# Summing the squares of the pre-norm on VectorE at all seven boundaries of a hybrid decoder trunk

## The reference

```python
def rms_norm(x, g):
    xf = x.astype(jnp.float32)
    y = xf * lax.rsqrt(jnp.mean(xf * xf, axis=-1, keepdims=True) + EPS)
    return (y * g.astype(jnp.float32)).astype(x.dtype)
...
    x = x + 0.5 * rms_norm(swiglu(rms_norm(x, f1_pre), f1_wg, f1_wu, f1_wd), f1_post)
    h = rms_norm(x, m_pre)
    z = h @ w_in            # three groups of channels: short conv, spatial gating, Conformer conv
...
    x = x + rms_norm(mix, m_post)
    x = x + 0.5 * rms_norm(swiglu(rms_norm(x, f2_pre), f2_wg, f2_wu, f2_wd), f2_post)
    gate = jax.nn.sigmoid(rms_norm(x, e_pre) @ e_wg)
    x = x + rms_norm(gate * (p @ e_wp), e_post)
```

## Time and profile before

| | |
|---|---|
| median of 3 runs | 2665.72 us (2664.89 to 2725.86) |
| profiled execution | 2664.45 us |
| its span, slowest core | 2662.7 us (cores 2655.2 to 2662.7) |
| granted clock, cores | 0.992 to 0.994 |
| PE, PEld busy | 2552.5, 1677.8 us |
| DVE, ACT, POOL busy | 1132.0, 1090.5, 613.8 us |

### The profile page before, as it was taken

The page is one execution under the profiler, slowest core; times in us unless marked ns, Lnnn a source line. Parts: engine busy times, 40 slices in busy tenths (PEclk is TensorE's granted clock), DMA queues, the critical chain, the costliest instruction groups (busy, mean ns, idle before and its releaser), DMA issues.

```text
span 2662.7 us, 52925 instructions; the slowest of 8 cores (2655.2 to 2662.7 us)
## 1 busy us (share of the span) xinstructions
PE 2552.5 (96%) x18352; PEld 1677.8 (63%) x18576; DVE 1132.0 (43%) x2680; ACT 1090.5 (41%) x2220; POOL 613.8 (23%) x943
## 2 busy tenths in 40 slices
PE   6999999999999999999999999999989999999996
PEld 3676565666566666666566765667656676566764
DVE  2222775215621368321662137722174215772237
ACT  3123673125611376322741237722274124761236
POOL 0052232004305223100420412400051222240014
PEclk9999999999999999999999999999999999999998
DMA  8354252434335524233655542533343444334341
GB/s 164 58 94 82 41 96 49 75 66 83 53 76 91 93 43 89 48 70 66 124 124 96 114 89 37 93 64 65 63 80 64 83 70 83 42 72 80 61 83 65
DMA packets 54595, 205.43 MB, mean 77 GB/s; under 512 B 10656, under 2 KB 23744, under 8 KB 39456
## 3 DMA queue, kind: packets, MB, share of 16 engines
q0 software_dynamic: 32608, 178.81, 38.2%
q1 hardware_dynamic: 21728, 23.23, 3.1%
HBM read 372.17 MB, written 9.63 MB: 143 GB/s over the span
## 4 chain that ended last, share of the span: by engine, by line
PE 90%; DVE 3%; ACT 3%; issue 3%; DMA 1%; POOL 1%; DVEq 0%; SPq 0%; ACTq 0%; POOLq 0%
PE PS L614 88%; PE PS L620 2%; ACT L490 1%; DVE XT L656 1%; ACT SCR L645 1%; DVE R L663 0%; ACT SQS L645 0%; DMA RING<-W 0%; DMA XT<-xT 0%; DVE SCR L663 0%; POOL R L651 0%; DVE SCR L656 0%; ACT R L645 0%; ACT PS L645 0%; POOL XT L656 0%
## 5 line engine op out<-in xcount | busy, mean ns | idle before, releaser
L614 PE MATMUL PS<-R,RING 128*128 128x256 bf16 (+2 forms) x10439 | 1602.3, 310 | 52.0 <-ACT SCR L645 23.9
L614 PEld LDWEIGHTS PS<-R,RING 128*128 128x128 bf16 x10560 | 1030.7, 98 | 556.1 <-issue 75.2
L645 ACT ACTIVATE SCR<-PS 128x256 f32<-128x256 f32 (+2 forms) x818 | 372.3, 463 | 965.6 <-PE PS L614 948.9
L614 PE MATMUL PS<-HIDR,RING 128*128 128x256 bf16 (+2 forms) x4934 | 752.8, 309 | 10.0 <-ACT SQS L645 3.5
L656 DVE TENSOR_TENSOR HIDR<-SCR,PS 128x512 bf16<-128x512 f32 (+2 forms) x552 | 282.3, 512 | 873.2 <-PE PS L614 856.5
L614 PEld LDWEIGHTS PS<-HIDR,RING 128*128 128x128 bf16 x4992 | 487.4, 98 | 252.3 <-issue 3.3
L685 POOL DMA_DIRECT2D RING<-W x192 | 106.5, 555 | 1585.7 <-PE PS L614 1526.8
L645 ACT ACTIVATE SQS<-PS 128x256 bf16<-128x256 f32 (+2 forms) x288 | 131.4, 456 | 436.9 <-PE PS L614 432.6
L656 POOL TENSOR_TENSOR XT<-XT,SCR 128x256 f32<-128x256 f32 (+2 forms) x221 | 206.0, 941 | 270.1 <-DVE SCR L663 246.0
L663 DVE SCALAR_TENSOR_TENSOR R<-XT,VECT,PS 128x256 bf16<-128x256 f32 (+2 forms) x368 | 186.0, 564 | 65.7 <-ACT PS L645 53.2
L490 ACT ACT_TABLE_LOAD x163 | 209.1, 1283 | 2.9
(11 more groups left out here) (92 smaller groups left out, 1063.4 us busy)
## 6 DMA issues: line engine op xcount, KB each, us to landing
RING<-W POOLq DMA_DIRECT2D x116, 1024.0 KB, 8.6
RING<-W POOLq DMA_DIRECT2D x64, 704.0 KB, 6.1
RING<-W POOLq DMA_DIRECT2D x8, 768.0 KB, 6.5
XT<-xT SPq DMA_DIRECT2D x8, 512.0 KB, 10.9
XT<-xT SPq DMA_DIRECT2D x16, 256.0 KB, 9.0
yT<-SCR SPq DMA_DIRECT2D x16, 256.0 KB, 3.2
yT<-SCR SPq DMA_DIRECT2D x32, 128.0 KB, 2.2
RING<-W POOLq DMA_DIRECT2D x4, 512.0 KB, 5.1
```

What stands on the lines that cost most here:

```text
L614: S.add("pe", lambda e: e.matmul(out.build(), lhsT.build(), rhs.build(), start=start, stop=stop), r=[lhsT, rhs], w=[out], dur=max(n, 64) / ...
L645: return e.activation(out=out.build(), in_=in_.build(), func=func, **k2)
```

## The change

`boundary` gets a parameter `fold`. All three places that call it (the feed-forwards, the mixer and the embedding stage) pass `fold=True`. Then block 0's square is left where it is; at block 1 DVE adds the squares of blocks 0 and 1 into the fp32 statistics bank in PSUM; at blocks 2 to 5 it adds the next square to that; at block 6 it adds the bank to block 6's square and writes the sum in bf16 over that square, and a ones-matmul of it starts the accumulation; block 7's square gets the second ones-matmul. So six adds on DVE stand in for six of eight matmuls on PE. The adds have the boundary's priority and can go to DVE only. The statistics bank is taken by the first add and no longer by the first matmul.

```diff
-        def boundary(si, ys, Y, gains, nxt, g, eps=EPS):
+        def boundary(si, ys, Y, gains, nxt, g, eps=EPS, fold=False):
...
                     SQ_(Hs(si, m), Xs(si, m), n, (1, g), tag="xsq")
-                    MM(bv(st2, 0, n), fx(ONESB[:]), Hs(si, m), n, m == 0, m == KC - 1, (0, g), acq=[st2] if m == 0 else (), tag="stat")
+                    A_ = bv(st2, 0, n)
+                    if not fold:
+                        MM(A_, fx(ONESB[:]), Hs(si, m), n, m == 0, m == KC - 1, (0, g), acq=[st2] if m == 0 else (), tag="stat")
+                    elif m == 1:
+                        TT_(A_, Hs(si, 0), Hs(si, 1), ALU.add, n, (1, g), acq=[st2], tag="xsum")
+                    elif 1 < m < KC - 2:
+                        TT_(A_, Hs(si, m), A_, ALU.add, n, (1, g), tag="xsum")
+                    elif m == KC - 2:
+                        TT_(Hs(si, m), Hs(si, m), A_, ALU.add, n, (1, g), tag="xsum")
+                        MM(A_, fx(ONESB[:]), Hs(si, m), n, True, False, (0, g), tag="stat")
+                    elif m == KC - 1:
+                        MM(A_, fx(ONESB[:]), Hs(si, m), n, False, True, (0, g), tag="stat")
...
-                boundary(si, ys, Ys, gains_post, nxt, downs[KC - 1].g + skew(si) + 0.5)
+                boundary(si, ys, Ys, gains_post, nxt, downs[KC - 1].g + skew(si) + 0.5, fold=True)
...
-                boundary(si, ys, Ys, lambda m, l=l: vec(l, G_MPOST + m), (l, G_F2PRE), wO[1].g + skew(si) + 0.5)
+                boundary(si, ys, Ys, lambda m, l=l: vec(l, G_MPOST + m), (l, G_F2PRE), wO[1].g + skew(si) + 0.5, fold=True)
...
-                boundary(si, ys, Ys2, lambda m, l=l: vec(l, G_EPOST + m), nxt, wG[1].g + sk + 0.5, 4.0 * EPS)
+                boundary(si, ys, Ys2, lambda m, l=l: vec(l, G_EPOST + m), nxt, wG[1].g + sk + 0.5, 4.0 * EPS, fold=True)
```

## The result

| | before | with the change |
|---|---|---|
| median | 2666.2 us | 2675.14 us |
| span of the profiled execution | 2662.7 us | 2673.7 us |
| granted clock of the cores, mean | 0.992 to 0.994 | 0.983 to 0.987 |

The ratio is 1.0033, 95% interval 1.0024 to 1.0042: some 9 us slower, where 5 us faster was forecast. Within 2% it is the same kernel, but the interval leaves no doubt of the sign, and the time lies just above the upper end of the range given (2675). In some executions the cores of a die ran at a lower granted clock and took longer, up to 3016 us here; the medians of this table are of all executions, while every ratio, and every time from here on, leaves such executions out.

What follows compares the result with a forecast made beforehand. It took sub-tile 0's DVE chain to bound the mixer and embedding boundaries, PE most other stretches. 36.8 us removed less 13.2, 6.6, 7.4 and 4.8 left 4.8 us less: 2661 us, range 2644 to 2675.

Steps and rivals of the forecast that it cites:

- my rest: At the boundaries, losses set against the removed matmuls: 13.2, 6.6, 7.4 and 4.8 us for the four kinds.
- the clock: Rival: longer waits at the four mixer boundaries lower the granted clock, some 1.4 us each, +6, 2667 us; chance 0.05.
- A matmul's price: At all boundaries, 0.216 us from start to start at 512 columns; removal gives at most 36.8 us.
- Lost matmuls: At boundaries in stretches where PE waits anyway, removed matmuls give nothing: 16 us of the 36.8.
- stalls by the adds: At boundaries, DVE adds delay PE: 2.0 us at each of six critical places, 0.5 in eight other stages.
- Mixer to second feed-forward: Four boundaries where sub-tile 0's chain already sets the end: loss 3.3 us each, 13.2 in all.
- Embedding to next feed-forward: Two boundaries before the next layer's first feed-forward, sub-tile 0's chain likewise critical: loss 3.3 us each, 6.6 in all.
- second feed-forward to embedding: Four boundaries; sub-tile 0 gains, sub-tiles 1 and 2 lose their 1.35 us plus 0.5 stall: loss 1.85 each, 7.4.
- first feed-forward to mixer: Four boundaries; sub-tile 0 hidden, half of 1.35 us lost plus 0.5 stall: loss 1.2 each, 4.8 in all.
- PE-bound after all: Rival: all adds fall into gaps or replace residual adds moved to POOL; 21 us gained, 2645 us; chance 0.22.
- DVE's queue sets the end: Rival at sub-tile 0's boundary: nothing moves, no gap is used; 3.7 us at six places, 2683 us; chance 0.22.
- The first add's contention: At each boundary's first add, two SBUF operands slow POOL by at most 1.05 us; 6.3 at six places, about cancelling.

Runs made afterwards that it cites:

- feed-forwards only: The change with squares summed on DVE only at the eight boundaries behind the feed-forwards, mixer and embedding keeping eight matmuls: 2655.02 us, 0.9963 of before.
- mixer only: The change with squares summed on DVE only at the four boundaries behind the mixer: 2678.29 us, 1.0051 of the kernel before.
- embedding only: The change with squares summed on DVE only at the two boundaries behind the embedding stage: 2667.74 us, 1.0011 of the kernel before.
- no adds: The change without its six adds, six of eight ones-matmuls still left out, so the statistic holds blocks 6 and 7 alone: 2634.50 us, 0.9866 of before.
- adds beside all matmuls: The change with all eight ones-matmuls kept and six adds into another bank that nobody reads: 2688.52 us, 1.0077 of the kernel before.
- mixer, sub-tile 0 only: The change with squares summed on DVE only behind the mixer and only for sub-tile 0: 2682.97 us, 1.0060 of the kernel before.
- the change with fillers: The change plus twelve unread ones-matmuls behind sub-tile 0's two statistic matmuls, after each mixer and embedding: 2662.69 us, 1.0006 of the kernel before.
- The opposite choice: The change with DVE sums only for sub-tile 0 behind feed-forwards and sub-tiles 1 and 2 behind mixer and embedding: 2641.14 us, 0.9919 of before.
- the chain put ahead in DVE's queue: The change with sub-tile 0's products, sums and adds into h behind a mixer ahead of other sub-tiles' work on DVE: 2687.47 us, 1.0079 of before.

## Why the prediction was wrong

The balance of spans, in us, with the clock loss and the rest as defined above; "my rest" is the loss that the prediction set against the same boundaries.

| kernel | span | removed | clock loss | rest | my rest |
|---|---|---|---|---|---|
| feed-forwards only | -8.7 | -21.0 | +2.4 | 9.9 | 12.2 |
| mixer only | +14.1 | -10.5 | +7.8 | 16.8 | 13.2 |
| embedding only | +4.4 | -5.3 | +2.1 | 7.6 | 6.6 |
| the change | +11.0 | -36.8 | +16.8 | 31.0 | 32.0 |
| no adds | -28.2 | -36.8 | +3.4 | 5.2 | 16.0 |
| adds beside all matmuls | +24.2 | 0 | +5.4 | 18.8 | 16.0 |
| mixer, sub-tile 0 only | +17.7 | -5.2 | +5.6 | 17.3 | |
| the change with fillers | -4.2 | -36.8 | +2.9 | 29.7 | |

By the means of the eight cores the rest is 8.1, 16.8 and 5.5 us for the three parts, 31.1 for the change, 5.4 without adds and 17.5 beside all matmuls.

**The step that failed is the clock.** The prediction's sum of waits and lost cover, 32.0 us, comes out (31.0, as a remainder); the 15.8 us between its span of 2657.9 and the measured 2673.7 are the clock loss of 16.8 less that 1.0. I had it as a rival, at 4 x 1.4 = 5.6 us and a chance of 0.05, sized from one stretch and independent of the waits that my own forecast lengthened. Both were mistakes. By my own terms the waits behind the four mixers would grow from about 1 to about 4 us, so a fall of the clock there belonged into the forecast, not into a rival. And 1.4 us is the loss in one stretch; behind the first mixer of the kernel after, the stretches at 380 and 404 us lose 1.7 and 2.0, and there are such places behind both embeddings and inside the embedding stage near 1344 us as well. That the fillers take back 13.9 us of it (10.8 by the means of the cores), and 11 us of the time, is the test of this. The Trainium skill has the mechanism (TensorE: Matmul & The Clock Gate, HAM oscillation — how this bites in real kernels): a kernel whose waits for operands make TensorE throttle pays again at half rate after each. The rows agree, with 0.51 behind a wait of 3.44 us and 0.50 behind one of 2.69, but not for every wait: the one of 2.94 us in the kernel before left the clock at 1.00.

**A matmul's price: right.** 36.8 us by the distance of 0.216 us. The opposite choice gained 16.5 to 26.9 us for 18.4 counted, and removal alone some 30 of 36.8 (interval 23 to 48). The busy means, 78 us, would have been far off; PE's busy time fell by 4.9 us only (50 or more were forecast), because it is a union of overlapping records, the slow clock stretches it, and the trace of before misses 224 of its 18576 matmuls.

**Lost matmuls: too high; stalls by the adds: too low.** I had split the 32.0 into 16 of matmuls in stretches that wait anyway and 16 of stalls. Without adds the rest is 5, not 16. The adds alone, beside all eight matmuls, make 19, and in the change they make 26 more than without them, for 16. The errors cancelled. That the sum came out is therefore partly luck.

**Mixer to second feed-forward: place and sign right, too small.** The wait before the first up matmul was forecast near 4 us and is 3.44, 3.44, 2.69 and 2.69. The stretch was to be 25 us long; it is 30:
```profile
372.90:402.85 29.95, 22.76 (x180) 17.29 (x177) 28.36 (x59) 20.53 (x54) 17.67 (x18) 0.91 0.49 94
```
It begins 3.2 us earlier, about what the one boundary ahead of it has saved (2.65), and ends 3.9 later. DVE is busy for 28.36 of 29.95 us, with 59 operations instead of 41. Its timeline shows how 3.7 us of adds can lengthen the chain by 4.6 (sub-tile 0 alone) to 7:
```profile
391.83 0.73 DVE L663 SCALAR_TENSOR_TENSOR SCR<-R,VECT,PS 128x512 f32<-128x512 f32 x1
392.49 0.43 DVE L656 TENSOR_TENSOR PS<-SQS,PS 128x272 f32<-128x272 bf16 x1
392.83 0.68 DVE L656 TENSOR_TENSOR PS<-R,PS 128x512 f32<-128x512 bf16 x1
393.43 0.42 DVE L656 TENSOR_TENSOR SQS<-SQS,PS 128x272 bf16<-128x272 bf16 x1
393.78 0.68 DVE L656 TENSOR_TENSOR PS<-R,PS 128x512 f32<-128x512 bf16 x1
394.38 0.41 DVE L656 TENSOR_TENSOR PS<-SQS,PS 128x256 f32<-128x256 bf16 x1
394.71 0.73 DVE L663 SCALAR_TENSOR_TENSOR SCR<-R,VECT,PS 128x512 f32<-128x512 f32 x1
```
Between two products of sub-tile 0 there now stand two of its own adds and three of the other sub-tiles' sums for the post-norm, which come due in the same stretch, and the product is held by the whole queue. Sub-tile 0's fourth product starts at 385.98 us and the last two at 396.91; before, they ran from 386.72 to 393.43. I had also let one of its two residual adds move to POOL (1.1 us); over the kernel 31 did, so that 84 instead of 115 are on DVE, but in this stretch the two of 512 columns stayed. A count over the whole kernel was right and the critical place got none of it. The gaps that were to take 0.6 us are filled: DVE waits for nothing before the four middle adds at 512 columns (0.0 in the group).

**Embedding to next feed-forward, second feed-forward to embedding, first feed-forward to mixer.** 7.6 us for 6.6 and 9.9 for 12.2: right within what a profile can tell.

**The rivals.** "PE-bound after all" falls. "DVE's queue sets the end" describes the place and the wait best; its price beyond the forecast was paid as clock and not as further waits. The point from which it decides, 2.8 us for the chain instead of 2.0, is passed at the mixer (4.6 measured in the kernel that changes nothing else).

**The first add's contention.** I had looked for it on POOL's side only, at 1.05 us and about cancelled. It fell on DVE (up to 2.77 us for 0.69), and it cost the change nothing, because at the six places that I had counted it the add took 0.69.

What stays open: how much of the 26 us by which the adds lengthen the rest falls on each stage, and what beside its length decides whether a wait pulls the clock down. The parts of the change add up to the whole within the errors (-9.4, +13.9 and +3.3 for +9; clock losses +12.3 for +16.8, by the means of the cores +13.7 for +14.5).

## What to carry to other kernels

Trading matmuls for vector work pays where the passing tile is covered by other tiles' matmuls, and costs where its chain is already the last to end; decide it per sub-tile and per boundary (here -22 us for the right ones, +9 for all, +18 for the worst four alone). Where the waits of PE grow in a place that is broken by waits already, put the microseconds after it at the half clock into the forecast (some 2 us in each such place here), and at every such place, not at one; look in the kernel's own rows for which waits did this and which did not. Before an operation with two SBUF operands is moved on DVE, look at what POOL does at the new place. And a free gap or a second engine counts only if it is there in the stretch that decides: read the count of operations between two steps of the chain, not the busy share of the span.

## What the runs showed of the hardware

- A wait of 3.44 us, behind a stretch in which PE was busy for 1.46 of 4 us, was followed by about 4 us at 0.51 of the clock; a wait of 2.94 us behind a stretch with 3.50 of 4 was not, and the clock stayed at 1.00. 2.6 us of matmuls without a purpose put into such waits at six places were worth 11 us of kernel time.
- An add on DVE with two SBUF operands took 0.69 us at 512 columns where POOL had no residual add, 1.49 to 2.77 us beside one or two residual adds of POOL, and 5.12 to 5.22 us beside five in a row, where it ended 0.56 us after the last; with one operand in PSUM its mean is 691 ns. POOL's residual adds of 512 columns became no slower in the change (mean 1337 ns before, 1303 after). The Trainium skill names the shared interface (GPSIMD Engine Reference, Architecture); the runs give it a price, and show that it depends on where the add stands: nothing in the change, and probably most of the 14 us that the chain put ahead in DVE's queue lost.
